# Moving the SiLU of four groups of convolved channel tiles between the rounds of the gate projection, in a two-layer SSD / HGRN2 / PEER trunk

## The reference

```python
z, xbc, dt = jnp.split(h @ w_in, [SSD_D_INNER, SSD_D_INNER + SSD_CONV_DIM], axis=-1)
xbc = jax.nn.silu(causal_depthwise_conv(xbc, conv_w, conv_b))   # 3072 channels, width 4
xs, bm, cm = jnp.split(xbc, [SSD_D_INNER, SSD_D_INNER + g * n], axis=-1)
dt = jax.nn.softplus(dt + dt_bias)
y = ssd_chunked_scan(xs, dt, a, bm, cm) + xs * d_skip
y = rmsnorm(y * jax.nn.silu(z), norm_g)                          # z: 2048 gate channels
return y @ w_out
```

## Time and profile before

| | us |
|---|---|
| median of 3 runs | 2456.57 |
| lowest and highest of them | 2453.83, 2457.74 |
| span of the profiled execution, first to last instruction | 2450.6 |
| PE busy | 2220.0 (91%) |
| POOL busy | 1483.6 (61%) |
| DVE busy | 1228.8 (50%) |
| ACT busy | 1192.8 (49%) |

### The profile page before, as it was taken

The page is one execution under the profiler, slowest core; times in us unless marked ns, Lnnn a source line. Parts: engine busy times, 40 slices in busy tenths (PEclk is TensorE's granted clock), DMA queues, the critical chain, the costliest instruction groups (busy, mean ns, idle before and its releaser), DMA issues.

```text
span 2450.6 us, 49827 instructions
## 1 busy us (share of the span) xinstructions
PE 2220.0 (91%) x17350; PEld 2162.8 (88%) x17353; DVE 1228.8 (50%) x2068; ACT 1192.8 (49%) x1785; POOL 1483.6 (61%) x776
## 2 busy tenths in 40 slices
PE   6797899999996789999988888999999767999998
PEld 6796799999995689999988878999999656999998
DVE  3987429920009974444435641994000798444443
ACT  3444354445447754444445434544444676444443
POOL 4560579888885544444447436789888655444443
PEclk9997999999997789999999989999999878999999
DMA  4340445555550035555534224455555101555553
GB/s 153 129 137 18 141 149 168 178 177 175 180 186 2 0 112 182 184 182 181 182 126 153 95 86 137 146 180 171 174 182 182 45 0 61 183 185 180 181 185 105
DMA packets 94558, 341.27 MB, mean 139 GB/s; under 512 B 10416, under 2 KB 11952, under 8 KB 94128
## 3 DMA queue, kind: packets, MB, share of 16 engines
q1 hardware_dynamic: 94512, 340.67, 42.5%
HBM read 339.58 MB, written 1.05 MB: 139 GB/s over the span
## 4 chain that ended last, share of the span: by engine, by line
PE 45%; issue 27%; POOL 19%; DVE 8%; DVEq 1%; POOLq 0%; ACT 0%; ACTq 0%
PE bank L998 30%; POOL wlo L374 18%; PE bank L707 12%; DVE oha L1419 6%; PE bank L979 2%; DVE big L1408 1%; DVEq L1419 1%; PE bank L747 0%; DVE big L1021 0%; POOLq L378 0%; POOLq L373 0%; ACT whi L438 0%; DVE rstd L1019 0%; DVEq L1406 0%; DVEq L1427 0%
## 5 line engine op out<-in xcount | busy, mean ns | idle before, releaser
L374 POOL TENSOR_TENSOR wlo<-raw,whi 128x1024 fp32r<-128x1024 f32 x384 | 965.3, 2520 | 426.8 <-ACT whi L438 426.0
L707 PE MATMUL bank<-hhi,whi 128*128 128x256 f32 x3072 | 880.0, 286 | 76.4 <-DVE hlo L1031 33.6
L438 ACT ACTIVATE whi<-raw 128x1024 fp32r<-128x1024 f32 x640 | 674.9, 1055 | 421.6 <-PE bank L998 379.6
L707 PE MATMUL bank<-hlo,whi 128*128 128x256 f32 x3072 | 874.9, 285 | 0.0
L707 PE MATMUL bank<-hhi,wlo 128*128 128x256 f32 x3072 | 874.7, 285 | 0.0
L707 PEld LDWEIGHTS bank<-hhi,whi 128*128 128x128 f32 x3072 | 596.0, 194 | 84.1 <-issue 66.1
L707 PEld LDWEIGHTS bank<-hlo,whi 128*128 128x128 f32 x3072 | 596.1, 194 | 0.1
L707 PEld LDWEIGHTS bank<-hhi,wlo 128*128 128x128 f32 x3072 | 595.5, 194 | 0.0
L426 POOL TENSOR_TENSOR hlo<-big,hhi 128x256 fp32r<-128x256 f32 x256 | 352.5, 1378 | 388.6 <-ACT hhi L675 388.6
L998 PE MATMUL bank<-hhi,whi 128*128 128x256 f32 x2048 | 579.7, 283 | 3.5 <-POOL hlo L426 3.5
L998 PE MATMUL bank<-hlo,whi 128*128 128x256 f32 x2048 | 579.6, 283 | 0.0
(11 more groups left out here) (204 smaller groups left out, 1552.0 us busy)
## 6 DMA issues: line engine op xcount, KB each, us to landing
raw<-w_u SPq DMA_DIRECT2D x256, 512.0 KB, 3.3
raw<-w_v SPq DMA_DIRECT2D x256, 512.0 KB, 3.3
raw<-w_ssd_in SPq DMA_DIRECT2D x40, 512.0 KB, 3.4
raw<-w_q SPq DMA_DIRECT2D x32, 512.0 KB, 3.4
raw<-w_hgrn_in SPq DMA_DIRECT2D x32, 512.0 KB, 3.3
raw<-w_ssd_out SPq DMA_DIRECT2D x16, 512.0 KB, 3.4
raw<-w_hgrn_out SPq DMA_DIRECT2D x8, 512.0 KB, 3.5
big<-keys SPq DMA_DIRECT2D x2, 1024.0 KB, 6.5
```

Of the source, the lines that this page charges most:

```text
L374: nc.gpsimd.tensor_tensor(wlo[:, r, :, :], raw[:, r, :, :], whi[:, r, :, :].bitcast(F32), ALU.subtract).then_inc(lo_pool, 1)
L438: nc.scalar.activation(whi[:, r, :, :], raw[:, r, :, :], ACT.Copy).then_inc(hi_done, 1)
L707: ins = nc.tensor.matmul(out, w[:, r, k, :], h[:, k, :], start=start and n == 0, stop=stop and n == 3 * KC - 1, **kw)
```

## The change

ACT's four SiLUs of quads 0 to 3, which stood together ahead of round 6, are spread out: rounds 6 to 9 are written out, and behind each of them stands one SiLU. Quads 4 and 5 stay where they were, behind round 9. No instruction is added or removed apart from the loop's own control, and no other engine's program changes.

```diff
             stream("ssd_in", copy_to(to_pad), 3, CONV // RAW)
             for q in range(CONV // 4 - 2):
+                stream("ssd_in", copy_to(lambda t: col(t - CONV)), CONV // RAW + q, CONV // RAW + q + 1)
                 conv_silu(q)
-            stream("ssd_in", copy_to(lambda t: col(t - CONV)), CONV // RAW)
             for q in range(CONV // 4 - 2, CONV // 4):
                 conv_silu(q)
             act.wait_ge(evac, SSD_TILES)
```

## The result

| | kernel before | changed kernel |
|---|---|---|
| median of 20 runs each, us | 2454.86 | 2458.28 |
| lowest, highest, us | 2449.84, 2461.33 | 2451.82, 2467.57 |
| ratio to the kernel before | | 1.0019, 95% interval 1.001 to 1.0028 |
| span of the profiled execution, us | 2450.6 | 2465.4 |
| mean granted TensorE clock in it | 0.949 | 0.938 |

The changed kernel is slower, by 0.19% in this set. Two later sets, with twelve runs of it in each, gave 1.0003 (0.9986 to 1.0019) and 1.0006 (0.9988 to 1.0024): less, but the intervals overlap with the first. In means it is 4.6 us slower in the first set (standard error 1.1), 1.3 and 1.6 us in the others (1.5 and 1.9), and 3.2 +- 0.8 us with the three weighted together. So some loss is there; its size isn't known well.

What follows compares the result with a forecast made beforehand. PE, 91% busy, was taken to stall on ACT, held by DVE's convolution. With the convolution then last, 1.6 us gained at L778 less about 0.1 behind it gave 2456.57 - 1.5 = 2455.1 us, range 2450.0 to 2459.5.

Steps and rivals of the forecast that it cites:

- The convolution becomes the last condition: Before L778: DVE's convolution, not the tile stream, ends last, quad 5 at 165.94 us; this forecast had 82%.
- a subtraction costs it 2.13 us: In DVE's convolution: each POOL subtraction adds 2.13 us to 6.42 us a quad, with 28 subtractions in all.
- The new wait before quad 2's SiLU: On ACT behind round 8: ACT stands 3 to 7 us for DVE before the SiLU of quad 2.
- quads 3 to 5 mostly at 6.4 us: Sign on DVE's timeline: the convolution's later quads run mostly at 6.4 us each if the forecast is right.
- The stream ended: End of the tile stream, tile 39 through: put at 149 us (146.4 to 152).
- L778 1.6 us earlier: Start of the scan's preparation: 167.1 us against 168.71, so 1.6 us gained there.
- I take no shift, as nothing says which way: TensorE's clock fall in L801: term set at 0, with 5 us less at best, 5.4 us more at worst.
- TensorE stays at 1.2 GHz: Rival at L778 to L801: low clock after PE's 18 us rest, 6.2 us slower, 2462.8 us; 6%.
- The sign of the total: Whole kernel: faster by 1.5 us, 2455.1 us against a median of 2456.57.
- The base: Starting time of the forecast: the 2456.57 us median of the kernel before, from which 1.5 us was taken.
- The half-speed matmuls behind the stall: PE's first 18 matmuls after its wait, at half clock: about 1.7 of the stream's 19.8 us gain.

Runs made afterwards that it cites:

- e3: Changed kernel with POOL's subtraction of the 16 gate tiles cut to 8 columns of one of 8 slices; 2439.49 us, ratio 0.9933.
- e4: Changed kernel with tap 0 of the convolution made by ACT from the PSUM bank instead of by DVE; 2447.93 us, ratio 0.9973.
- e2: Changed kernel with 76 zero matmuls on PE behind tile 39, so PE hardly rests before L778; 2451.91 us, ratio 0.9996.
- e6: Changed kernel with two copies on ACT, 1.5 us in all, between quad 5's end and its SiLU; 2455.7 us, ratio 1.0004.
- cut kernels: Kernels ended behind the first mixer with a norm and store; means: before 306.6, changed 307.4, with zero matmuls 305.4, with ACT delay 306.0 us.
- e7: Changed kernel with convolution tap 0 on ACT and 12 gate-tile subtractions (rounds 7 to 9) on DVE, not POOL; 2436.67 us, ratio 0.9923.

## Why the prediction was right or wrong

- **The convolution becomes the last condition; a subtraction costs it 2.13 us: right.** 98.26 us for six quads and 28 subtractions, 98.2 forecast; e3 confirms the term by taking the subtractions away, and e4 that the convolution ends last. By the rule of the Trainium skill ("SBUF — State Buffer", "Who interferes with whom"), with the full 2.5 us each, it would have been 38.5 + 28 x 2.5 = 108.5, an estimate that the trace doesn't bear out. Each held instruction does end behind POOL's, as the rule says; but it lasts some 2.6 us in all and would have taken 0.48 anyway, which leaves 2.13. The prediction gave another reason, that the held instruction begins shortly ahead; mostly it begins behind (0.03 us ahead to 0.36 behind). And it named only instructions with two SBUF inputs, while L1108, with one, was held as long.
- **The new wait before quad 2's SiLU, 3 to 7 us: right, at the lower edge,** 2.96, and it cost nothing, as the convolution ended later still. Of the signs named, "quads 3 to 5 mostly at 6.4 us" holds for two of them. The stream ended at 150.9 - 1.75 = 149.2, forecast 149.
- **L778 1.6 us earlier: right.** Counted from the clock's first return, 137.8 to 138.2 against 139.6 to 139.9.
- **"I take no shift, as nothing says which way": this step failed.** The clock's fall in L801 was priced as a scatter around no change. It is not scatter: the fall stood at 153.6 in all five traces of the kernel before and at 150.2 in all six of the changed one, and moving L801 by 1.5 us moved it from one to the other. That term was put at 0 and measures +1.75 to +2.1 us, which eats the gain of 1.5. The trace of before had the two numbers (L801 from 177.2, fall at 182.6); what it couldn't show is that the fall doesn't follow L801.
- **The rival "TensorE stays at 1.2 GHz": wrong in its mechanism.** The clock was back at 174.2 in the changed kernel. The rest costs 0.45 us between L778 and L801 (e2), where this rival had 5.4 + 2.3, and where it was kept but L801 moved back (e6) there was no loss in L801.
- **The sign of the total.** Forecast 1.5 us less, measured 3.4 more in medians of the first set, 0.3 and 3.2 in the others (3.2 +- 0.8 in means). The failed step explains why the gain isn't there. The mixer as a whole gives 0.8 +- 0.45 us of loss (cut kernels): nothing in the half of the runs that end early, some 2 us in the other half (3.8 in the traces). The rest, about 2.4 us, stays open: the later stages differ by up to 10 us between traces of the same kernel, and whether the change makes the long ones more frequent there was not settled.
- **The base.** The three runs shown had a median 1.7 us above that of the twenty; the forecast of 2455.1 was a difference put on a high base. From the twenty's 2454.86 it would have been 2453.4.
- **Smaller points.** The half-speed matmuls behind the stall cost 2.0 us (18 of them in 3.96 us), not 1.7. And the measured 2458.28 lies inside the range given, 2450.0 to 2459.5, because that range had room for the scatter of the runs and for an earlier fall; the forecast itself pointed the other way.

## What to carry to other kernels

Before a wait is removed, ask what the waiting gave to the engine that now ends last: here POOL's pause was most of DVE's free time, and its cost per subtraction could be read from quads with different counts. A gain of 1 to 2 us ahead of a stage in which TensorE's clock falls can be swallowed whole, as here; compare several traces from a mark of the clock, and count matmuls at each level. Where one engine's work holds another, moving that work to the held engine can pay (1.23 us instead of 2.13): here it brought 11 us (e7 against e4), where reordering ACT brought nothing.

## What was not expected of the hardware

- The falls of the granted clock keep fixed places in this kernel's own time: 153.6 or 150.2 us behind the first return, in 15 traces from several chips, while the first return itself lay between 27.8 and 30.9 us. That return follows the projection's first matmul (L707) by 4.2 to 5.8 us, and the first L1111 follows the return by 41.8 to 42.7, in every trace, so the clock's places and the kernel's stages keep together. Why they do isn't shown. The Trainium skill, "TensorE: Matmul & The Clock Gate", Part 1, says that what watches the activity runs freely and doesn't start with the kernel; the traces agree in that the fall ignores where L801 begins. What they add is that, counted from the first return, the place did not vary from run to run of the same kernel.
- The delay in e6 cost nothing in the mixer: 1.5 us of added work on the path, and it ended at 259.8 and not at 261.4.
- A subtraction of 128 x 1024 on DVE took 1.23 us, on POOL 2.35 to 2.67, of which DVE lost 2.13. Of the two, only DVE was held: POOL's took as long beside the convolution as behind it (2.35 to 2.65 us and 2.38 to 2.66 in the changed kernel).
